# Attention keys produced already turned, minima in place of negated maxima, and a reordered start of the head loop, in a two-layer decoder trunk

## What is computed

```
lat = h @ w_in                          # 256 x 672: 384 query latents, 256 key/value latents, 32 rotated
c_q, c_kv, k_rope = split(lat)          # c_q and c_kv are then RMS-normed
q  = (c_q @ w_uq)   -> 16 heads x 96    # 64 plain + 32 rotated
kv = (c_kv @ w_ukv) -> 16 heads x (64 keys + 64 values)
q_rope, k_rope = rope(q_rope), rope(k_rope)      # k_rope is one for all heads
s = (q_nope . k_nope + q_rope . k_rope) * 96**-0.5, masked causally
o = softmax(s) @ v ;  out = o @ w_o
```

## Time and profile before

| what | value |
|---|---|
| median of 3 runs (lowest, highest) | 1304.67 us (1304.33, 1304.68) |
| the profiled execution, its own time | 1304.9 us |
| its span, first to last instruction | 1303.1 us |
| granted TensorE clock, mean | 1.000 |
| PE busy | 1298.2 us (100%) |
| DVE busy | 649.2 us (50%) |
| ACT busy | 287.8 us (22%) |
| POOL busy | 86.9 us (7%) |
| chain that ended last | PE 98%, ACT 1%, DMA 1% |

### The profile page before, as it was taken

The page is one execution under the profiler, slowest core; times in us unless marked ns, Lnnn a source line. Parts: engine busy times, 40 slices in busy tenths (PEclk is TensorE's granted clock), DMA queues, the critical chain, the costliest instruction groups (busy, mean ns, idle before and its releaser), DMA issues.

```text
span 1303.1 us, 25215 instructions
## 1 busy us (share of the span) xinstructions
PE 1298.2 (100%) x10760; PEld 852.5 (65%) x10760; DVE 649.2 (50%) x1471; ACT 287.8 (22%) x432; POOL 86.9 (7%) x116
## 2 busy tenths in 40 slices
PE   9999999999999999999999999999999999999998
PEld 5878888888997444555555555555555555555555
DVE  5888666666887344233433533423343353342436
ACT  4874444433694000010010010001001001000102
POOL 3401111111002110000000000000000000000100
PEclk9999999999999999999999999999999999999999
DMA  8625555556369999999999999999999999999992
GB/s 304 253 105 173 193 192 193 193 193 210 120 249 378 358 416 406 421 409 414 419 408 416 419 420 405 419 419 405 405 420 410 403 420 421 411 413 419 419 411 101
DMA packets 124423, 441.92 MB, mean 339 GB/s; under 512 B 7346, under 2 KB 18052, under 8 KB 109732
## 3 DMA queue, kind: packets, MB, share of 16 engines
q1 hardware_dynamic: 119696, 424.57, 82.5%
q0 software_dynamic: 4560, 15.85, 3.4%
q10 hardware_dynamic: 68, 0.02, 0.0%
HBM read 430.84 MB, written 9.57 MB: 338 GB/s over the span
## 4 chain that ended last, share of the span: by engine, by line
PE 98%; ACT 1%; DMA 1%; SPq 0%; issue 0%; DVE 0%
PE psum L1663 67%; PE psum L441 9%; PE psum L443 8%; PE psum L442 8%; PE psum L1210 1%; PE psum L1669 1%; DMA raw<-in_mla_w_in 1%; PE psum L1317 0%; ACT w_hi L412 0%; PE psum L1305 0%; PE psum L1326 0%; PE psum L1341 0%; PE psum L1316 0%; PE psum L1615 0%; PE psum L1428 0%; PE psum L457 0%
## 5 line engine op out<-in xcount | busy, mean ns | idle before, releaser
L1663 PE MATMUL psum<-raw_more,hT 128*32 128x512 f32 x1656 | 535.7, 592 | 0.0
L1663 PE MATMUL psum<-raw,hT 128*32 128x512 f32 x1032 | 334.6, 592 | 0.0
L1663 PE MATMUL psum<-raw_more,xg_odd 128*32 128x512 f32 x1680 | 245.4, 592 | 0.0
L1663 PE MATMUL psum<-raw_more,xg 128*32 128x512 f32 x1704 | 241.8, 592 | 0.1
L2473 DVE STREAM_TRANSPOSE hT<-hid 32x128 f32<-32x128 f32 x672 | 206.2, 307 | 10.3
L2463 DVE SCALAR_TENSOR_TENSOR hid<-hid,psum 96x512 f32<-96x512 f32 x55 | 37.6, 683 | 302.7 <-PE psum L1663 301.9
L1154 ACT ACTIVATE hid<-psum 96x1024 f32<-96x1024 f32 (+1 forms) x32 | 29.2, 914 | 663.8 <-PE psum L1663 474.2
L1663 PEld LDWEIGHTS psum<-raw_more,hT 128*32 128x32 f32 x1656 | 154.3, 110 | 32.0 <-issue 32.0
L1663 PEld LDWEIGHTS psum<-raw_more,xg_odd 128*32 128x32 f32 x1680 | 84.5, 110 | 98.0 <-issue 98.0
L1663 PEld LDWEIGHTS psum<-raw_more,xg 128*32 128x32 f32 x1704 | 83.4, 110 | 98.2 <-issue 97.8
L1663 PE MATMUL psum<-raw,xg_odd 128*32 128x512 f32 x1008 | 147.7, 592 | 0.0
(11 more groups left out here) (368 smaller groups left out, 1352.6 us busy)
## 6 DMA issues: line engine op xcount, KB each, us to landing
raw_more<-in_moe_w_gate SPq DMA_DIRECT2D x71, 1024.0 KB, 18.4
raw_more<-in_moe_w_up SPq DMA_DIRECT2D x70, 1024.0 KB, 18.6
raw_more<-in_moe_w_down SPq DMA_DIRECT2D x69, 1024.0 KB, 17.7
raw<-in_moe_w_down SPq DMA_DIRECT2D x43, 1024.0 KB, 18.0
raw<-in_moe_w_up SPq DMA_DIRECT2D x42, 1024.0 KB, 17.5
raw<-in_moe_w_gate SPq DMA_DIRECT2D x41, 1024.0 KB, 18.3
raw<-in_ffn_w_gate SPq DMA_DIRECT2D x14, 1024.0 KB, 5.2
raw<-in_ffn_w_up SPq DMA_DIRECT2D x14, 1024.0 KB, 5.3
```

What stands on the lines that cost most here:

```text
L1663: return pe.matmul(psum[rows_q, bank, cols], stationary, moving, start=start, stop=stop, tile_position=(0, rows_q.start), skip_group_check ...
```

## The change

It does five things.

- The unit of `w_ukv` is split with its columns regrouped, all keys first and then all values (two instructions per unit on ACT and two on DVE, in place of one each). The key products are made with weights as the stationary operand, so that keys come out turned (64 key columns on partitions, 256 tokens along the row), two heads to a matmul: four units of 12 matmuls of 256 columns for keys, four units of 6 matmuls of 512 columns for values. The copies out of PSUM multiply the keys by minus the scale. ACT copies two key units (two instructions of 64 x 512 each) and four value units (one of 128 x 512 each); DVE copies the last two key units.
- The heads no longer transpose k: two transposes in place of four, and `qk_copy` copies 256 columns in place of 512.
- The scores being negated and scaled, DVE takes minima with a mask of plus BIG. The result is the bias of Exp as it stands: the multiplication L2047 and the `link` waits go, and each half of `exps` waits for its own minimum.
- The rotated 32 key columns are turned by PE (two transposes between the query products of tile 1), copied by ACT, and spread over the 16 heads by three DMAs on SP's queue, SBUF to SBUF, 15 times 32 partitions x 1 KB in all. POOL's two copies into `k` go. The scores of head 0 wait for the DMAs.
- On ACT, `kv_copy(4)` and `qk_copy(0)` come ahead of the table load, and the high part of the last `w_o` unit is written in four quarters in steps 6, 8, 10 and 12. On DVE, the second `kv_copy` moves from step 4 to step 5, behind `maxima`.

The diff, cut to its core:

```diff
-        KV_ORDER = [(t, b) for b in range(4) for t in range(TT)]
+        KV_BANKS = [0, 1, 4, 5, 6, 7, 6, 7]
+        KV_UNITS = [(KEYS, 0), (KEYS, 1), (VALUES, 0, 0), (VALUES, 1, 0), (VALUES, 0, 1), (VALUES, 1, 1),
+                    (KEYS, 2), (KEYS, 3)]
...
@@ block.sync
             for s in range(SLOTS - 1):
                 load(sp, (s, FFN_BASE + 1), ffn_v[s // 2][0, s % 2, 0])
+                if s == 1:
+                    sp.wait_ge(q_copied, KEY_ROPE)
+                    for dst, n in ((kT_first[0][NOPE:QK, 1:2], 1), (kT_first[1][NOPE:QK], 2),
+                                   (kT[NOPE:QK], HEADS - 4)):
+                        sp.dma_start(dst, kT_first[0][NOPE:QK, 0:1].broadcast_to([ROPE, n, T])
+                                     ).then_inc(x_first_then_rope, 16)
@@ block.gpsimd
-            for t in range(TT):
-                pool.tensor_copy(k[:, t, :, NOPE:QK],
-                                 latent[:, t, QR + KVR:LAT].unsqueeze(1).broadcast_to([P, HEADS, ROPE])
-                                 ).then_inc(qk_ready, 1)
@@ block.scalar
+            def key_rope():
+                act.wait_ge(c_ps, 2 * TT + 1)
+                act.activation(kT_first[0][NOPE:QK, 0], psum[0:ROPE, 1, T:2 * T], ACT.Copy, scale=-SCALE).then_inc(q_copied, 1)
...
-            for n in range(2, 4):
+            for n in range(2, 5):
                 kv_copy(n)
-            act.activation(half[:, 1:2], half[:, 0:1], ACT.Exp)
-            kv_copy(4)
             def qk_copy(h):
-                copy(qkT[0:QK, h % 2, :], psum[0:QK, h % 2, :]).then_inc(qkT_ready, 1)
+                copy(qT[0:QK, h % 2, :], psum[0:QK, h % 2, 0:T]).then_inc(qkT_ready, 1)
             def exps(h):
-                act.wait_ge(max_ready, h + 1)
                 for r, (c0, c1) in enumerate([(0, P), (P, 3 * P)]):
-                    act.activation(probs[:, b, c0:c1], probs[:, b, c0:c1], ACT.Exp, scale=SCALE,
+                    act.wait_ge(max_ready, 2 * h + r + 1)
+                    act.activation(probs[:, b, c0:c1], probs[:, b, c0:c1], ACT.Exp, scale=-1.0,
...
                 if i == 0:
-                    split_hi(act, mla_use(W_O + 3))
+                    act.activation(half[:, 1:2], half[:, 0:1], ACT.Exp)
                     kv_copy(5)
...
+                if i in (6, 8, 10, 12):
+                    last_high(i // 2 - 3)
@@ block.tensor
+                    if t == 1 and b == 1:
+                        turn_key_rope()
...
-                for n, src in enumerate([q[:, 0, h], q[:, 1, h], k[:, 0, h], k[:, 1, h]]):
-                    mm = pe.transpose(psum[0:QK, h % 2, n * P:(n + 1) * P], src, ident[:])
+                for t in range(TT):
+                    mm = pe.transpose(psum[0:QK, h % 2, t * P:(t + 1) * P], q[:, t, h], ident[:])
...
                 if h == 0:
-                    pe.wait_ge(q_copied, 3 * TT)
+                    pe.wait_ge(q_copied, 3 * TT + 1)
+                    pe.wait_ge(x_first_then_rope, 16 * 4)
@@ block.vector
-                dve.tensor_copy(k[:, t, 4 * b:4 * b + 4, 0:NOPE], src[:, :, 0:NOPE]).then_inc(kv_copied_v, 1)
-                dve.tensor_copy(v[...], src[:, :, NOPE:NOPE + V]).then_inc(kv_copied_v, 1)
+                for e in range(2):
+                    dve.tensor_scalar(key_pairs(KV_UNITS[n][1], e),
+                                      psum[e * NOPE:(e + 1) * NOPE, KV_BANKS[n]].rearrange("p (g t) -> p g t", t=T),
+                                      -SCALE, None, ALU.mult).then_inc(kv_copied_v, 1)
...
-                    link(dve.tensor_tensor_reduce(..., -BIG, ALU.add, ALU.max, mx[:, 2 * b + r:2 * b + r + 1]))
-                dve.tensor_scalar(nmx[:, 2 * b:2 * b + 2], mx[:, 2 * b:2 * b + 2], -SCALE, None,
-                                  ALU.mult).then_inc(max_ready, 1)
+                    dve.tensor_tensor_reduce(..., BIG, ALU.add, ALU.min,
+                                             nmx[:, 2 * b + r:2 * b + r + 1]).then_inc(max_ready, 1)
```

More of the change, by code:

```diff
@@ L885, in _ @@
             latents(1)
-            split_hi(act, mla_use(W_UKV), UKV)
-            split_hi(act, mla_use(W_UKV + 1), UKV)
+            for a in range(KVR // P):
+                s, n = mla_use(W_UKV + a)
+                act.wait_ge(landed[s], n * 16)
+                act.wait_ge(used[s], n - 1)
+                for w in range(2):
+                    ins = act.activation(keys_first(w_hi, s)[:, w], by_head(raw, s)[:, w], ACT.Copy)
+                ins.then_inc(hi_done[s], 1)
             c_high(1)
             def kv_copy(n):
-                t, b = KV_ORDER[n]
                 act.wait_ge(kv_ps, n + 1)
[L892 to L895, removed]
+                bank = psum[:, KV_BANKS[n]]
+                if KV_UNITS[n][0] == KEYS:
+                    for e in range(2):
+                        act.activation(key_pairs(KV_UNITS[n][1], e), bank[e * NOPE:(e + 1) * NOPE].rearrange(
+                            "p (g t) -> p g t", t=T), ACT.Copy, scale=-SCALE).then_inc(kv_copied_a, 1)
+                else:
+                    _, t, b = KV_UNITS[n]
+                    copy(v[:, t, b * BANK:(b + 1) * BANK], bank).then_inc(kv_copied_a, 1)
             q_copy(0)
@@ L931, in o_high, with last_high @@
                 copy(xTh_mla[:, g, :], psum[:, 6 + g % 2, 0:T]).then_inc(o_hi, 1)
+            def last_high(n):
+                s, use = mla_use(W_O + 3)
+                cols = slice(n * BANK, (n + 1) * BANK)
+                if n == 0:
+                    act.wait_ge(landed[s], use * 16)
+                    act.wait_ge(used[s], use - 1)
+                ins = act.activation(w_hi[:, s, cols], raw[:, s, cols], ACT.Copy)
+                if n == 3:
+                    ins.then_inc(hi_done[s], 1)
             for i in range(HEADS + 7):
@@ new lines, in up_kv @@
+                k0 = QR // P
+                if KV_UNITS[n][0] == KEYS:
+                    for e in range(2):
+                        g = 2 * KV_UNITS[n][1] + e
+                        terms = []
+                        for a, (s, _) in enumerate(w_units):
+                            pair = [w[:, s, g * P:(g + 1) * P] for w in (w_hi, w_lo)]
+                            terms.append((pair[0], pair[1], c_hi[:, k0 + a, :], c_lo[:, k0 + a, :]))
+                        marks = {}
+                        if e == 1 and n == len(KV_UNITS) - 1:
+                            marks = {a: used[s] for a, (s, _) in enumerate(w_units)}
+                        elif e == 1:
+                            marks = {len(terms) - 1: kv_ps}
+                        product(pe, psum[:, KV_BANKS[n], e * T:(e + 1) * T], terms, marks=marks,
+                                units=units if e == 0 else {})
+                else:
+                    _, t, b = KV_UNITS[n]
+                    tok = slice(t * P, (t + 1) * P)
+                    terms = []
+                    for a, (s, _) in enumerate(w_units):
+                        vals = [w[:, s, HEADS * NOPE + b * BANK:HEADS * NOPE + (b + 1) * BANK] for w in (w_hi, w_lo)]
+                        terms.append((c_hi[:, k0 + a, tok], c_lo[:, k0 + a, tok], vals[0], vals[1]))
+                    product(pe, psum[:, KV_BANKS[n]], terms,
+                            marks={len(terms) - 1: kv_ps})
@@ L1381, in _ @@
                 if i < HEADS:
-                    transpose_qk(i)
+                    transpose_q(i)
                 else:
```

142 lines of the change are left out of this document (84 added, 58 removed).

## The result

The changed kernel takes 1308.14 us (median of 10 runs, 1306.21 to 1310.70), the kernel before, run beside it, 1304.83 us (1304.26 to 1305.35, 10 runs): a ratio of 1.0025 [1.0017, 1.0034], 3.3 us slower. That is past the range (1301.1 to 1304.8), on the side of the fourth rival, late DMAs. The runs of the changed kernel also lie 4.5 us apart, those of the kernel before 1.1 us. The profiled execution after took 1307.69 us, its span 1305.9.

What follows compares the result with a forecast made beforehand. PE bounds the whole span; in the steady head loop ACT is the limit, DVE close behind. Start 1.0 plus loop 0.6 made 1.6 us, forecasting 1303.1 us, range 1301.1 to 1304.8.

Steps and rivals of the forecast that it cites:

- the fourth rival: Slow 1 KB pieces land late and PE stands at head 0's scores; 1314 at 0.5 us a piece; chance 0.07.
- SP's DMAs: Transfers spreading the rotated keys: issue by 39.7, landing between 47.5 and 50.5, taken as 49; no cost, high end 0.5 us.
- the free way: On the DMA queue: loads ahead of the spreading DMAs would have drained, leaving the way free near 45.5.
- From 50.1 on every microsecond costs one: At head 0's scores: each microsecond of DMA landing past 50.1 adds one; slower by over 0.2% past 54.3.
- The start: Up to the first transposed probabilities: 55.5 in place of 56.51, a gain of 1.0 us.
- PE is there before that: At head 3's scores: PE ready before DVE is done at 53.43, with 1.1 us of key transposes less.
- The pair of reductions: DVE's two reductions for minima at the start: 0.72 us in place of 1.03, without multiplication and waits.
- The third rival: The start gives nothing: POOL takes gaps between DVE's halves, or DVE's copies take 0.7 us; 1304.2; chance 0.23.
- The loop: Head loop, steps 4 to 16: ACT's savings less the quarters give 0.5, plus 0.1 for short waits, 0.6 us gained.
- rounds of 3.4 us after step 12: Late head loop: sign of being right, two-head rounds of about 3.4 us, against about 3.8 while the quarters run.
- The second rival: The quarters hide in ACT's gaps in the loop; 3.0 us gained in sum, 1301.7, or 1301.0; chance 0.25.
- The table load: ACT's 1.28 us load at the start, moved behind head 0's copy: costed at nothing.

Runs made afterwards that it cites:

- e1_rope_first: The changed kernel with SP's three spreading DMAs issued ahead of both w_gate loads: 1304.18 us, ratio 0.9998.
- e11_busy_64: The changed kernel with 64 small matmuls on zeros on PE in front of the wait for the DMAs: 1307.81 us, ratio 1.0024.
- after_again: The changed kernel as it is, measured and profiled a second time: 1307.22 us, ratio 1.0018.
- e8_split_step3: On top of e1_rope_first, the last w_o unit's high part in one piece at the end of step 3 on ACT: 1303.35 us, ratio 0.9989.
- e4_busy: The changed kernel with 24 small matmuls on zeros on PE in front of the wait for the DMAs: 1307.18 us, ratio 1.0017.
- e5_later: The changed kernel with the three spreading DMAs one load later on SP's queue, behind another 1 MB load: 1311.38 us, ratio 1.0051.
- e2_head1: The changed kernel with the wait for the three DMAs moved from head 0's scores to head 1's: 1304.42 us, ratio 0.9998.

## Why the prediction was wrong, by its steps

**SP's DMAs: the step that failed.** The prediction put the issue at 39.7, the landing at 49 with bounds of 47.5 and 50.5, and the cost at 0 to 0.5 us. The first issue was right (39.32); the last and largest DMA went out at 40.70. Its landing was at 51.3 in one profile and 52.6 in another. The bounds were built from a free way near 45.5 and bytes or packets of the transfer. The size of the transfer held: 3.9 us to land with the queue free (e1_rope_first). The step that failed is the free way. From 46 to 48 the rate falls to 194 GB/s at full share, which is where the pieces seem to move, and from 48 to 50 it is back at 351. But the last DMA's signal came 3 us later than that, at 51.26, while later loads were already moving. The three DMAs issued into this filled queue took 6.4, 7.4 and 10.6 us to land, the loads around them 8.4 to 12.1. The trace of before had this row and it was not read (DMA issues of before, 30 to 60 us):

```profile
raw<-in_ffn_w_gate SPq DMA_DIRECT2D x2, 1024.0 KB, 8.7
```

The second gate load of before is issued at 38.2 and lands near 47, later than the way was taken to be free. This is a warning and not a rule: in the change the 32 and the 64 KB landed at 45.7 and 47.4, before the gate load issued ahead of them (38.91, landed at 49.1). Where in the 10.6 us each piece of the last DMA waited, none of the traces shows. The fourth rival (chance 0.07) had the outcome and the sign, PE idle with a DMA as releaser, but put it on slow pieces, which e1_rope_first refutes.

**What a wait costs: the second step.** "From 50.1 on every microsecond costs one" left out the clock. From the anchor, the first minimum came at 25.37 in the change and 23.04 in e1_rope_first, 2.33 us of wait; from there to the transposed probabilities it took another 1.30 us longer. Together 3.63 us, of which about 1.1 are the clock's, shown by e11_busy_64 against after_again. With 4.2 us late as its mark for a slowdown of 0.2%, the rival also needed a landing at 54.3; with landings of 51.3 and 52.6 the two profiled executions took 1307.7 and 1309.4 us, because the gains to be eaten up were smaller than 1.6 us as well.

**The start: 1.0 us predicted, 0.46 to 0.49 measured** in the kernels without a wait (28.51 and 28.48 against 28.97). The clock times looked like a hit, 55.43 against a forecast of 55.5, but 0.62 us of that is where the two executions stood at the anchor. The step that failed is "PE is there before that". The timeline of DVE in e1_rope_first:

```profile
49.96 0.28 DVE L2135 CUSTOM_DVE_ANT_0 res<-psum,mask 128x128 f32<-128x128 f32 x1
...
51.13 1.41 DVE L2124 TENSOR_SCALAR kT<-psum 64x512 f32<-64x512 f32 x2 [0.54 <-PE psum L467]
52.57 0.29 DVE L2135 CUSTOM_DVE_ANT_0 res<-psum,mask 128x128 f32<-128x128 f32 x1
```

DVE stands 0.54 us until PE has the key unit, which took 1.53 us (49.30 to 50.83) and not 1.44, and the two key copies then take 1.44 us, not 1.22. The pair of reductions was better than taken (0.63 and 0.56 us for 0.72), and so was the first minimum (0.31 us earlier than the first maximum before, for 0.12).

**DVE's low parts and POOL.** The third rival's mechanism, gaps for POOL between the halves, happened and cost nothing in the end. Four halves took 5.75 us and one whole low part beside POOL 2.83, 8.4 us from 33.13 to the rotation at 41.55, against 7.6 before (33.71 to 41.33). But POOL, which came into more gaps, was done with the queries 17.0 us from the anchor (at 44.0) in place of 17.6 (45.1), and DVE's last three rotation instructions took 0.42 us each. The timeline of DVE in the change:

```profile
44.31 0.42 DVE L2109 TENSOR_TENSOR q<-gain_mla 128x256 f32<-128x256 f32 x1
44.77 0.42 DVE L2110 TENSOR_TENSOR gain_mla<-q,trig 128x256 f32<-128x256 f32 x1
45.23 0.43 DVE L2111 TENSOR_TENSOR q<-gain_mla 128x256 f32<-128x256 f32 x1
45.57 4.49 DVE L442 TENSOR_TENSOR w_lo<-raw,w_hi 128x2048 fp32r<-128x2048 f32 x2
```

Before, they took 0.85, 0.85 and 0.72. So 0.8 us were lost, 0.7 came back in the rotation and 0.4 in the two low parts (4.49 us for 4.90; the prediction had 0.34). The Trainium skill (SBUF - State Buffer, Who interferes with whom) has DVE with two SBUF inputs and a reading GpSimd shut each other out whole, and the trace agrees: 0.42 us once POOL was through, 0.72 to 0.85 beside it. The time lent to POOL came back.

**The loop: 0.6 us predicted, 0.12 measured** (27.91 against 28.03). With the quarters running ACT is busy without idle time, as predicted, but a quarter takes a slot of 0.52 us, not 0.47. The timeline of ACT in the change:

```profile
64.01 0.63 ACT L974 ACTIVATE w_hi<-raw 128x512 fp32r<-128x512 f32 x1
64.53 0.38 ACT L850 ACTIVATE gain_mla<-psum 96x256 f32<-96x256 f32 x1
```

The 0.47 was that of a copy out of PSUM; this one reads SBUF. And the rounds of 3.4 us after step 12 never came: from there on e1_rope_first needs 3.59 and 3.74 us a round where before needed 3.67 and 3.73. The sum credited ACT's savings of steps 13 to 16, where PE already sets the pace. Without the quarters most rounds are 3.5 to 3.6, not 3.4: PE then waits about 0.2 us for DVE's normalized probabilities, and ACT is no longer what binds. The second rival's claim, that the quarters would hide, is wrong, since e8_split_step3 gains 1 us in the loop by moving them.

**The table load** at nothing fits the trace of e1_rope_first, where head 0's queries are copied at 48.27, before it (48.67), and PE goes on; no run moved it back.

So the change is two things: some 0.5 us of gain in the median (e1_rope_first against before, itself no more than this kernel's measurement can tell), and 3.0 to 4.0 us of loss in the medians (3.63 in the profiles, from the anchor) by the order of one queue. With the DMAs first and the last high part in ACT's gap at step 3 the kernel takes 1303.35 us, less than either; both such kernels have intervals that end just under 1, at 0.1% gained.

## What to carry to other kernels

A small DMA that compute waits for goes ahead of the bulk loads on its queue, even at the price of starting those later; its landing is better guessed from how long the loads of the same stretch take to land (here 8.4 to 12.1 us) than from its bytes alone. If it cannot go first, let its wait stand as late as the data allow, since here a stall of PE of 2.0 to 3.5 us cost another 1.1 us in clock. When two profiles are laid side by side, take an event ahead of the change as the anchor before calling half a microsecond a gain, and when work is moved off an engine's full stretch, look for the place where that engine stands waiting, not for the place where it has the most slack on average.

## What the runs showed that was not expected

- Three DMAs with 480 KB in all, in pieces of 1 KB onto 32 partitions: the last one takes 3.9 us to land with nothing else ahead of them, 10.6 to 11.7 with bulk loads ahead, issued at the same moment.
- While these pieces move, the DMA engines are fully busy at about half of the rate: 194 GB/s at a share of 1.10, against 382 to 412 of the bulk loads. The Trainium skill (SBUF - State Buffer, Door 1: The DMA port swizzle) has a transfer whose partitions span 32 reach only half of the ports; the trace agrees with it, though no run here tells the 32 partitions from the pieces of 1 KB.
- PE's granted clock fell after a single idle stretch of 2.0 us (e4_busy, 0.50 from 54 to 56), 2.4 (the change), 3.5 (after_again) and 5.3 us (e5_later), and was back at 1.00 some 3.5 to 5 us after PE was fed again. It stayed at 1.00 over one of 0.46 us (e2_head1).
- The landing of such a DMA varies by more than 1 us from run to run, and a kernel that waits for it inherits this: 4.5 and 3.9 us between its runs, 1.4 with the wait covered.
